# Host-side layouts for the inputs and a pairwise modulation head in a two-block transformer kernel

## What is computed

```python
cond, cond_ctx = silu(c), silu(c_ctx)
sh, sc, gt = split(cond @ w_mod[i] + b_mod[i], 3)          # the same with cond_ctx for ctx
h_lat = x * (1 + sc) + sh;  h_ctx = ctx * (1 + sc_c) + sh_c
# layer 0, MLA: h @ w_in is split into q_down (256), kv_down (128), k_rope (64), gate (2048)
qn = rmsnorm(q_down); ckv = rmsnorm(kv_down); attention over 16 heads; y = (o * silu(gate)) @ w_out
x = layernorm(alpha * x + gt * y)
# layer 1, S5: a diagonal complex state space over 128 groups of 16 channels and 64 states, both directions
lam_bar = exp(lam * dt);  b_bar = (lam_bar - 1) / lam * b;  x_t = lam_bar * x_{t-1} + b_bar u_t;  y = Re(c x)
```

## Time and profile before

| | |
|---|---|
| median of three runs | 1820.68 us (1819.55 to 1823.26) |
| the profiled execution | 1816.69 us, its span 1814.7 us |
| PE busy | 1628.8 us, 90% of the span |
| DVE, ACT, POOL busy | 634.1, 411.8, 626.4 us |
| mean granted clock of TensorE | 0.959 of 2.4 GHz |

### The profile page before, as it was taken

The page is one execution under the profiler, slowest core; times in us unless marked ns, Lnnn a source line. Parts: engine busy times, 40 slices in busy tenths (PEclk is TensorE's granted clock), DMA queues, the critical chain, the costliest instruction groups (busy, mean ns, idle before and its releaser), DMA issues.

```text
span 1814.7 us, 26957 instructions
## 1 busy us (share of the span) xinstructions
PE 1628.8 (90%) x10616; PEld 1212.6 (67%) x10616; DVE 634.1 (35%) x1224; ACT 411.8 (23%) x907; POOL 626.4 (35%) x614
## 2 busy tenths in 40 slices
PE   3889999999999949996878799999989997999997
PEld 3454455555544448875767688888878786888786
DVE  4772656655630061245766100001131113233301
ACT  1423332323310020024545300000121001244300
POOL 0014999999899999941111000000000000000000
PEclk9899999999999969998989899999999999999999
DMA  8949767886888857569998544544333341444441
GB/s 263 284 119 277 251 123 185 219 184 173 202 199 189 191 118 173 160 253 270 328 313 252 176 154 147 161 140 139 128 104 117 119 136 52 134 142 159 133 142 50
DMA packets 232013, 320.28 MB, mean 176 GB/s; under 512 B 30994, under 2 KB 201589, under 8 KB 227189
## 3 DMA queue, kind: packets, MB, share of 16 engines
q1 hardware_dynamic: 194496, 223.37, 38.9%
q0 software_dynamic: 34096, 86.96, 21.2%
q10 hardware_dynamic: 3333, 8.71, 1.3%
HBM read 266.67 MB, written 52.30 MB: 176 GB/s over the span
## 4 chain that ended last, share of the span: by engine, by line
PE 77%; DMA 9%; DVE 6%; ACT 4%; issue 3%; SPq 1%; POOL 0%; DVEq 0%; ACTq 0%; POOLq 0%; PEldq 0%
PE bank L842 36%; PE bank L1168 12%; PE bank L1040 6%; DMA arena<-s_responses 4%; DMA s_responses<-arena 2%; PE bank L909 2%; PE bank L1224 2%; PE bank L973 1%; PE bank L942 1%; PE bank L941 1%; PE bank L939 1%; PE bank L940 1%; PE bank L937 1%; PE bank L810 1%; PE bank L936 1%
## 5 line engine op out<-in xcount | busy, mean ns | idle before, releaser
L842 PE MATMUL bank<-ht,ring 128*128 128x256 f32 (+1 forms) x1408 | 364.8, 422 | 9.8 <-DVE ht L2168 9.0
L842 PEld LDWEIGHTS bank<-ht,ring 128*128 128x128 f32 x1408 | 270.4, 192 | 102.3 <-issue 70.1
L1168 PE MATMUL bank<-arena,ring 128*128 128x256 f32 x1024 | 222.9, 381 | 1.1 <-PEq L1159 1.1
L1168 PEld LDWEIGHTS bank<-arena,ring 128*128 128x128 f32 x1024 | 195.6, 191 | 28.0 <-issue 1.2
L842 PE MATMUL bank<-gate,ring 128*128 128x256 f32 (+1 forms) x640 | 194.9, 467 | 4.9 <-DVE gate L2221 3.4
L842 PEld LDWEIGHTS bank<-gate,ring 128*128 128x128 f32 x640 | 122.4, 192 | 76.8 <-issue 63.1
L1040 PE MATMUL bank<-ring,ht 128*128 128x256 f32 x512 | 113.8, 384 | 18.6 <-DVE ht L1817 18.6
L1040 PEld LDWEIGHTS bank<-ring,ht 128*128 128x128 f32 x512 | 98.3, 193 | 32.6 <-issue 18.9
L842 PE MATMUL bank<-arena,ring 128*128 128x256 f32 x480 | 107.8, 388 | 3.9 <-DVE arena L2283 3.9
L842 PEld LDWEIGHTS bank<-arena,ring 128*128 128x128 f32 x480 | 93.8, 196 | 17.8 <-DVE arena L2283 4.3
L2140 DVE SCALAR_TENSOR_TENSOR gate<-bank,col,gate 128x256 f32<-128x256 f32 x16 | 7.7, 481 | 198.0 <-ACT gate L1600 198.0
(11 more groups left out here) (366 smaller groups left out, 2434.1 us busy)
## 6 DMA issues: line engine op xcount, KB each, us to landing
ring<-in_s_w_glu SPq DMA_DIRECT2D x32, 1024.0 KB, 5.3
ring<-in_w_mod SPq DMA_DIRECT2D x24, 1024.0 KB, 8.8
ring<-in_w_up SPq DMA_DIRECT2D x22, 1024.0 KB, 5.1
arena<-s_b_rows POOLq DMA_DIRECT2D x32, 512.0 KB, 11.4
arena<-s_power_rows POOLq DMA_DIRECT2D x32, 512.0 KB, 11.6
s_b_powers<-arena POOLq DMA_DIRECT2D x32, 512.0 KB, 3.1
s_c_powers<-arena POOLq DMA_DIRECT2D x32, 512.0 KB, 5.3
ring<-in_s_w_in SPq DMA_DIRECT2D x16, 1024.0 KB, 7.8
```

What stands on the lines that cost most here:

```text
L842: mm = pe.matmul(psum[2 * (u % 2) + m][:, 0:mv.free_size()], ring[:, sl, k, m * P:(m + 1) * P], mv, start=(kg == 0 and k == 0), stop=(kg = ...
L1168: mm = pe.matmul(psum[4 * par + 2 * (s // 2) + m][:, 0:S], ring[:, sl, k, m * P:(m + 1) * P], yt[:, kg * 8 + k, :], start=(kg == 0 and k = ...
```

## The change

- The host lays out x, ctx, the vectors (`vecs`), S5 parameters (`s5_pars`, with log_dt repeated for each state), d, b and c in the order in which the kernel wants them, w_mod[0]'s first eight slots and the head weights with one contiguous run of 8 KB or 16 KB for each partition. All input transposes on PE and their copies go. c is read by POOL straight from the input; the sign of the imaginary part moves from c to b's columns and into the adds and subtracts of S5.
- Modulation slots come as pairs (shift and scale of the same 256 channels), in banks 6 and 7 in turn; after each pair DVE transposes 128x128, adds the bias and modulates its two tiles, ACT the same for ctx. The head has its weights in a place of their own (2 MB, outside the ring), and runs in four pieces of two channel tiles; its four banks accumulate over the pieces.
- ACT copies and squares the head's results. `angles` and `trig` move behind the columns; `s5_columns` stands behind one gate unit, not two. exp(log_dt) is worked out on 128x128, not 128x2.
- SP's first loads: vectors, two modulation slots, ctx, x, two slots, head weights, four slots, b, then the gate weights. The constants go to ACT's queue.

```diff
@@ SP
-            sp.dma_start(cst[:, :], a["consts"]).then_inc(const_in, 16)
...
-            for s in range(NSLOT):
-                load(s, rows8(wm[0], 0, s * MT2))
-            sp.dma_start(xtok[:, 0:2, :], a["ctx"].rearrange("b (t p) d -> p (b t) d", p=P)).then_inc(x_in, 16)
-            sp.dma_start(xtok[:, 2:4, :], a["x"].rearrange("b (t p) d -> p (b t) d", p=P)).then_inc(x_in, 16)
-            for s in range(NSLOT, 2 * NSLOT):
-                sp.wait_ge(slot_done, s - NSLOT + 1)
-                load(s % NSLOT, rows8(wm[0], 0, s * MT2))
+            def load_mod(s):
+                sp.dma_start(ring[:, s % NSLOT].rearrange("p k m -> p (k m)"), a["w_mod_0"][s // 2 + s % 2 * 4])\
+                    .then_inc(w_in_[s % NSLOT], 16)
+            sp.dma_start(col[:, :], a["vecs"]).then_inc(vec_in, 16)
+            for s in range(2):
+                load_mod(s)
+            sp.dma_start(xc[:, :, :].rearrange("p k t -> p (k t)"), a["ctx"]).then_inc(x_in, 16)
+            sp.dma_start(xl[:, :, :].rearrange("p k t -> p (k t)"), a["x"]).then_inc(x_in, 16)
+            for s in range(2, 4):
+                load_mod(s)
+            sp.dma_start(head_w.rearrange("p u k m -> p (u k m)"), a["mla_w_head"]).then_inc(head_w_in, 16)
+            for s in range(4, 8):
+                sp.wait_ge(slot_done, s - 3)
+                load_mod(s)
+            sp.dma_start(bcol.rearrange("p z q c -> p (z q c)"), a["s5_b"]).then_inc(b_in, 16)
@@ PE
...
+            def modulation_pair(p):
+                if p >= 2:
+                    pe.wait_ge(mod_set, p - 1)
+                for s in (2 * p, 2 * p + 1):
+                    pe.wait_ge(w_in_[s % NSLOT], 16 * (s // NSLOT + 1))
+                    modulation(psum[6 + p % 2], s % 2 * (MT2 // 4), s % NSLOT)
+            def head(p):
+                for k in (2 * p, 2 * p + 1):
+                    pe.wait_ge(h_ctx, k + 1)
+                    pe.wait_ge(h_lat, k + 1)
+                    for s in range(2):
+                        for m in range(2):
+                            M = ROPE if s == 1 and m == 1 else P
+                            mm = pe.matmul(psum[2 * s + m][0:M, :], head_w[:, s, k, m * P:m * P + M], ht[:, k, :],
+                                           start=(k == 0), stop=(k == KD - 1))
...
+            modulation_pair(0)
+            modulation_pair(1)
+            pe.wait_ge(head_w_in, 16)
+            head(0)
+            for p in range(2, 4):
+                modulation_pair(p)
+                head(p - 1)
+            head(3)
...
-            linear("mla_gate", 1, 2, lambda k: ht[:, k, :])
+            linear("mla_gate", 1, 1, lambda k: ht[:, k, :])
             s5_columns()
-            linear("mla_gate", 1, 2, lambda k: ht[:, k, :], first=2)
+            linear("mla_gate", 1, 3, lambda k: ht[:, k, :], first=1)
@@ ACT
+            act.wait_ge(x_in, 32)
+            for k in range(KD):
+                act.wait_ge(mod_set, k // 2 + 1)
+                modulate(0, k)
+            for j in range(2):
+                act.wait_ge(head_done, j + 1)
+                act.copy(qd[:, j, :], psum[j][:, :]).then_inc(qkv_copied, 1)
+                act.activation(sq1[:, j, :], psum[j][:, :], ACT.Square).then_inc(sq_set, 1)
...
-            trigs = ((), (), (6, 7, 8), (9, 10, 11), (12, 13), (14, 15), (), ())
+            trigs = ((), (0, 1, 2), (3, 4, 5, 6), (7, 8, 9), (10, 11), (12, 13), (14, 15), ())
             for s in range(8):
+                if s == 0:
+                    act.wait_ge(b_scaled, 1)
                 if s == 4:
+                    act.wait_ge(b_spilled, 4 * 16)
@@ DVE
+            def modulation_pair(p):
...
+                dve.wait_ge(slot_done, 2 * p + 2)
+                link(dve.transpose(t.rearrange("p m j -> p (m j)"), psum[6 + p % 2][:, 0:P]))
+                link(tt(mod[:, 0, 2 * p:2 * p + 2, :], t[:, 0:2, 0:2], sh, ALU.add))
+                stt(out=mod[:, 0, KD + 2 * p:KD + 2 * p + 2, :], in0=t[:, 2:4, 0:2], scalar=1.0, in1=sc, op0=ALU.add, op1=ALU.add)\
+                    .then_inc(mod_set, 1)
+                dve.wait_ge(mod_set, p + 1)
+                dve.wait_ge(x_in, 32)
+                for k in (2 * p, 2 * p + 1):
+                    modulate(0, k)
...
+            modulation_pair(0)
             dve.wait_ge(act_tanh, 1)
...
+            modulation_pair(1)
...
             cmul(2, 1, 1, 1)
             cmul(3, 2, 1, 2)
+            modulation_pair(2)
             cmul(5, 4, 1, 4)
+            modulation_pair(3)
...
+            dve.wait_ge(par_got, 5)
+            dve.wait_ge(b_in, 16)
@@ POOL
-            for n, v in enumerate((bcol, ccol)):
-                for z in range(2):
...
-                pool.dma_start(gen_c[b % 2].rearrange("p z d q c -> p (z d q c)"), spill_bc[:, b, 1, :]).then_inc(gen_c_in[b % 2], 16)
+                pool.dma_start(gen_c[b % 2].rearrange("p z d q c -> p (z d q c)"), a["s5_c"][:, b, :]).then_inc(gen_c_in[b % 2], 16)
```

More of the change, by code:

```diff
@@ L274, in program @@
         trig_near = before_heads(2, BLK, NC5)
[L275 removed]
+        trig_out = [before_heads(2, 2, BLK, NC5) for _ in range(3)]
         assert before_heads.at <= at_prob
[L277 to L284 removed]
+        trig_angle += [carve(22304 + 512 * i, 2, BLK, NC5) for i in range(2)]
         before_prob = Carver(at_prob)
@@ L448, in program @@
         cp_stored = sem("cp_stored")
-        trig_stored = [sem(f"trig{i}_stored") for i in range(2)]
+        trig_stored = [sem(f"trig{i}_stored") for i in range(3)]
         bm_in = [sem(f"bm_in{i}") for i in range(2)]
@@ L668, in _ @@
                 load_b(b)
-                sp.wait_ge(trig_stored[b], 16 * (NB5 // 2))
+                for i in range(3):
+                    sp.wait_ge(trig_stored[i], 16 * len(range(i, NB5, 3)))
                 load_trig(b)
@@ L1332, in _ @@
             link(act.activation(pars[7], pars[5], ACT.Abs))
+            act.wait_ge(const_in, 16)
             act.activation(pars[7], pars[7], ACT.Sin, scale=-0.5, bias=half_pi).then_inc(act_trig, 1)
[L1335 to L1343 removed]
@@ new lines, in _ @@
+            act.wait_ge(head_done, 3)
+            act.copy(kvd, psum[2][:, :]).then_inc(qkv_copied, 1)
+            act.activation(sq1[:, 2, :], psum[2][:, :], ACT.Square).then_inc(sq_set, 1)
+            act.wait_ge(head_done, 4)
+            for h in range(2):
+                act.copy(kr[h * ROPE:(h + 1) * ROPE, :], psum[3][0:ROPE, :]).then_inc(qkv_copied, 1)
+            act.wait_ge(qkv_copied, 5)
+            act.wait_ge(sq_set, 3)
+            act.sem_inc(unit_free[1 - unit_at["mla_head"] % 2], 2)
@@ L1481, in _ @@
             act.wait_ge(ln_norm, 1)
-            act.wait_ge(mod_set, 2)
-            modulate(1)
+            act.wait_ge(mod_set, 5)
+            for k in range(KD):
+                modulate(1, k)
             act.wait_ge(h_ctx, 2 * KD)
@@ L1921, in _ @@
                 dve.tensor_copy(o, psum[4 + f % 4][:, :]).then_inc(colt_set, 1)
-            dve.wait_ge(bc_spilled, 8 * 16)
-            for b in range(10, NB5):
+            dve.wait_ge(const_in, 16)
+            for b in range(10):
                 angles(b)
@@ L1936, in _ @@
             tt(kr_rot, kr_rot, rot_t, ALU.add).then_inc(normed, 1)
+            for b in range(10, NB5):
+                angles(b)
             def rope(pair, d0):
@@ L2055, in _ @@
             dve.wait_ge(ln_norm, 2)
-            dve.wait_ge(mod_set, 2)
-            modulate(1)
+            dve.wait_ge(mod_set, 5)
+            for k in range(KD):
+                modulate(1, k)
             dve.wait_ge(h_lat, 2 * KD)
@@ L2114, in scan @@
                 link.upto(2)
-                for z, (p, m, op) in enumerate(((t1, t2, ALU.subtract), (t3, t4, ALU.add))):
+                for z, (p, m, op) in enumerate(((t1, t2, ALU.add), (t3, t4, ALU.subtract))):
                     o = x5[par][z]
```

377 lines of the change are left out of this document (118 added, 259 removed), and 4 rows, old and new, of the table _INS.

## The result

The changed kernel took 1791.03 us in the median of 4 runs (1790.04 to 1797.57), the kernel before 1821.97 beside it (4 runs); the ratio is 0.9836, interval 0.9815 to 0.9857. That is 31 us faster where 43 were forecast. 1791 lies at the upper edge of the range (1766 to 1792), 13 above the predicted 1777.7; of the three outcomes with chances it was "faster". The profiled execution took 1790.04, its span 1787.9.

What follows compares the result with a forecast made beforehand. PE bounds the kernel, so its waits count. A first head pair 43.0 us earlier, later stages unchanged and POOL's tables at cost 0, taken off the median 1820.68, gave 1777.7 us; range 1766 to 1792.

Steps and rivals of the forecast that it cites:

- Part 1: Prologue loads: the head starts when 9.39 MB have landed at 409 GB/s, plus 0.5 for completion, at 26.0 us.
- Part 2: Head to gate: 27.5 for the same 32 matmuls, 4.1 for modulation slots, 2.2 for low clock; ends at 59.8, against 80.8.
- Part 3: Between head and gate: b and c transposes go, 21.8 us; columns ready 72.7, wanted 73.5; last trig store lands by 177.
- Part 5: POOL's tables: start near 108, last store near 727, PE's u projection ends at 754; slack grows from 12 to 27; cost 0.
- Part 4: Rest of the prologue, gate to first head pair: unchanged at 120.6 us, first pair at 180.4, 43.0 us earlier.
- every later stage of the length it has: Sign of being right, for everything from the first head pair on: attention and later stages keep their lengths, at no cost.
- the slow pairs: Rival in the attention, pairs slowed by POOL's passes: all seven slow 4.6 us longer (1782), all quick 4.2 shorter; no chance given.
- the 5 us that the prediction gave as a sign of being wrong: Sign of error: the attention or S5 stage changes length by over 5 us.
- DMA at the old rate: Rival at the first loads: head and everything behind it 3.9 us later, 1781.6; chance 0.2.
- The clock in the interleaved head: Rival in the head: modulation passes keep PE at 1.2 GHz until the gate, 29.4 us more, 1807; chance 0.05.
- POOL as the end: Rival at S5's start: tables beginning as late as now hold S5, 1817; chance 0.05, with removed stalls returning elsewhere.
- Slower: Rival before attention: PE at the low clock through head, gate and statistics, 148 us more, about 1926; chance 0.03.

Runs made afterwards that it cites:

- experiment 5: Changed kernel with the head's fourth matmul 128 columns wide and head weights in two transfers, the second awaited only ahead of the third head piece: 1787.14 us.
- experiment 2: Changed kernel with POOL's first table held until PE has done the first gate units after the columns: 1782.74 us, ratio 0.979 to the kernel before.
- experiment 8: Changed kernel with POOL's first table held until PE has done six gate units: 1807.64 us.
- experiments 11 and 12: Both kernels run once more, unaltered, for second profiles: changed kernel 1789.66 us, ratio 0.9828; kernel before 1823.2 us.
- experiment 10: Changed kernel with full-width head, split head weights, five repeated POOL passes before its first table, POOL stopped ahead of block 13 for the layer norm: 1772.74 us, ratio 0.9727.

## Why the prediction was off, point by point

- **Part 1**, head start 26.0: 26.8. That the landing of these bytes decides is right, shown by experiment 5. That the number is so near is in part luck: DMA moved 420 GB/s from 2.5 to 26.8, not 409, but that is 10.2 MB, not 9.39. Slots 4 and 5 had been issued at 9.87 and 12.49, long before the head weights landed, and moved beside them. The 0.5 for completion stands on no row.
- **Part 2**, 27.5 for "the same 32 matmuls": wrong by 2.3. The order of the work was changed from one bank after another to all four banks for each k, and with it the number of width switches, from one pair of them to eight. The prediction counted matmuls and did not look at their shapes. The 2.2 charged for the low clock held as a sum: the first piece took 9.90 and the second 7.55, 2.35 apart. But the granted clock reads 1.00 in both. The matmuls' own times show half speed all the same: the first six records start 0.85 to 1.01 us apart, up to 31.2, and from 32 on 0.43 to 0.53. In the kernel before the first five started 0.85 to 0.98 apart, up to 54.65, and there the granted clock read 0.50. So the slow start is there, and the granted clock of this profile does not show it; why it doesn't stays open.
- **Part 3**, the cover of 0.8 at the columns: held, PE asked at 77.15 and DVE was done. The transposes' 21.8 went in full. What failed is "its store, 5.7 us in the earlier trace rows, lands by 177, ahead of the last silu at 179": it landed at 184.5. The angles were taken at their length without POOL, while Part 5 had just moved POOL's start 60 us forward, onto them. The price is 1.2 us, shown by experiment 2.
- **Part 4**: right; from the gate's start to the last gate unit 119.0 were forecast and 119.0 measured, then 2.9 in place of 1.6.
- **Part 5**, first table 108, last store 727: 103.9 and 727.4. Right, and POOL's finish is no bound. But the slack was misread (experiment 8), and the table start was treated as harmless.
- **The attention, "every later stage of the length it has"**: the main step that failed. "From 223.37 on the work and its order are the same", so it stands in the sum at nothing, and the slow pairs at up to 4.6 in a rival. It cost 8.8 and 4.0; the first is over the 5 us that the prediction gave as a sign of being wrong. Of this the lock took 3.0 and 4.2 (pairs 2 to 7), which is the rival, with its size about right: five and six of six pairs ran at 37.6 to 37.9 where three had. So the prediction named the mechanism and left it out of its sum. That the phase is not drawn once but held, because two periods are near each other, was not seen, and so neither was that an earlier lock is a sure cost. The earlier trace rows gave the two lengths, 36.7 for one pair and 37.8 for a later one; that it never goes back shows in the list of all pairs (experiments 11 and 12). The other 5.8 of the first profile, in the ends of the attention, had no term, and their cause stays open.
- **The other rivals.** DMA at the old rate fell (414 and more). The clock in the interleaved head fell: granted 1.00 from 26.8 to the gate, and records 0.43 to 0.53 apart from 32 on. POOL as the end did not occur, experiment 8 shows what it would have been: 1807.6. Slower fell.
- **Sum**, by the first profiles: 43.0, less 0.8, 2.6 (2.3 the switches), 1.2 in the prologue, 8.8 attention, 2.7 behind it, is 26.9; by the second ones, with 4.0 in the attention and 2.2 behind it, 31.9. So the prologue's own misses (4.7) weigh as much as the attention's 4.0 to 8.8. The 2 to 3 behind the attention are within what two executions of one program differ by there (7), and their cause stays open.

## What to carry to other kernels

When a change shifts a long side job against a loop, compare their periods: here two that lie 1.15 us apart, about the length of one pass, locked, and a delay of the side engine by 20 us (experiment 2) or a stop of 14 us (experiment 10) gained time, as long as its slack held. "The same matmuls in another order" cost the same here only with tile widths that change as seldom; padding the narrow one with zero weights gave the time back. Read the slack of a producer at its consumer's first instruction, loads included, not at its last store.

## What was not expected of the hardware

- A 64-column matmul amid 128-column ones cost more than a 128-column one (3.78 against 3.48 us for the group of four), though eight of them in a row ran as fast as the wide ones.
- Matmuls at half speed for 4.4 us under a granted clock of 1.00, at the head's start.
- With fewer POOL passes two attention pairs were 5 us longer, with waits for a load; one pass more in each block made pairs 2 to 7 together 4 to 5 us shorter.
- DVE's eight 128x256 modulations took 2.8 us with POOL stopped and 6.0 to 10.3 beside its passes; beside the two 5.4 us scalings single 128x512 operations took 4.6 and 6.0 in place of 0.7 and 0.4.
